# Expert loop of a two-block layer: token gather by quarter rows, turned on VectorE, with scatter and pair down halves in turns

## The reference, cut to what matters

```python
def moe(h, w_router, router_bias, w_gate, w_up, w_down, ws_gate, ws_up, ws_down):
    ...
    scores = jax.nn.sigmoid(xt.astype(jnp.float32) @ w_router.astype(jnp.float32))
    ...
    _, eidx = lax.top_k(jnp.where(emask, sel, -jnp.inf), TOP_K)
    ...
    gates = jnp.einsum('mk,mke->me', wts, jax.nn.one_hot(eidx, N_EXPERTS, dtype=wts.dtype)).astype(h.dtype)

    def expert_block(args):
        x_b, g_b = args
        hg = jnp.einsum('td,edf->tef', x_b, w_gate)
        hu = jnp.einsum('td,edf->tef', x_b, w_up)
        return jnp.einsum('tef,efd->td', jax.nn.silu(hg) * hu * g_b[..., None], w_down)
    ...
    shared = (jax.nn.silu(xt @ ws_gate) * (xt @ ws_up)) @ ws_down
    return (routed.reshape(M, D) + shared).reshape(B, T, D)
```

## Time and profile before

| what | us |
|---|---|
| median of 3 runs (1544.88 to 1546.15) | 1545.85 |
| span of the profiled execution | 1536.5 |
| median less span (what lies around it) | 9.35 |
| expert loop's repeated part, 15 starts of `pair_in` apart (862.00 to 1505.61) | 643.61 |
| one step of it, mean | 42.91 |

### The profile page before, as it was taken

One profiled execution on the slowest core, in us unless ns is written; L12 is line 12 of the kernel. 1 busy time (PEld: TensorE's weight loads), 2 busy tenths in 40 slices (PEclk: granted clock), 3 DMA queues, 4 the chain that ended last, 5 costly groups with the idle time before them and its releaser, 6 DMA issues. The chain is left out here.

```text
span 1536.5 us, 30699 instructions
## 1 busy us (share of the span) xinstructions
PE 1452.9 (95%) x12703; PEld 1211.8 (79%) x12703; DVE 935.7 (61%) x1479; ACT 660.6 (43%) x943; POOL 146.2 (10%) x254
## 2 busy tenths in 40 slices
PE   6999989999999999978898999999999999999996
PEld 5997878789999999866697677777777777777773
DVE  5653666366776368546767466666656555666564
ACT  4333522346443356615555433444444433344442
POOL 8000000001000001001121011110110111110000
PEclk9999999999999999889999999999999999999998
DMA  7455110254554668435617788899888888899883
GB/s 268 141 205 171 58 62 4 79 196 165 198 187 165 163 122 182 151 108 192 213 36 303 286 331 324 336 354 348 333 343 315 314 341 325 326 355 349 336 335 142
DMA packets 115851, 351.99 MB, mean 229 GB/s; under 512 B 9689, under 2 KB 35504, under 8 KB 99328
## 3 DMA queue, kind: packets, MB, share of 16 engines
q1 hardware_dynamic: 105536, 317.85, 57.5%
q0 software_dynamic: 8064, 26.88, 5.6%
q10 hardware_dynamic: 2112, 5.31, 1.0%
HBM read 346.73 MB, written 3.28 MB: 228 GB/s over the span
## 5 line engine op out<-in xcount | busy, mean ns | idle before, releaser
L3411 DVE TENSOR_TENSOR weights_lo<-raw_weights,weights_hi 128x2048 fp32r<-128x2048 f32 x97 | 219.3, 2288 | 77.6 <-ACT weights_hi L3295 77.6
L3295 ACT ACTIVATE weights_hi<-raw_weights 128x2048 fp32r<-128x2048 f32 x97 | 181.8, 1910 | 20.9 <-DMA raw_weights<-in_w_gate 18.7
L3064 PE MATMUL bank<-x_hi,weights_hi 128*128 128x256 f32 x544 | 154.2, 284 | 1.2 <-DVE weights_lo L3411 1.2
L3065 PE MATMUL bank<-x_lo,weights_hi 128*128 128x256 f32 x544 | 153.9, 283 | 0.0
L3066 PE MATMUL bank<-x_hi,weights_lo 128*128 128x256 f32 x544 | 153.9, 283 | 0.0
L371 PE MATMUL bank<-in_x_hi,in_w_hi 128*128 128x272 f32 (+2 forms) x392 | 116.4, 297 | 3.5 <-DVE in_w_lo L320 3.5
L371 PE MATMUL bank<-in_x_hi,in_w_lo 128*128 128x272 f32 (+2 forms) x392 | 114.2, 291 | 0.0
L371 PE MATMUL bank<-in_x_lo,in_w_hi 128*128 128x272 f32 (+2 forms) x392 | 114.1, 291 | 0.0
L3153 PE MATMUL bank<-raw_weights,gathered_pair 128*64 128x512 f32 x512 | 113.4, 595 | 0.0
L1447 DVE TENSOR_TENSOR ffn_weights_lo<-weight_ring,ffn_weights_hi 128x2048 fp32r<-128x2048 f32 x33 | 75.6, 2292 | 51.9 <-ACT ffn_weights_hi L1442 51.9
L3064 PEld LDWEIGHTS bank<-x_hi,weights_hi 128*128 128x128 f32 x544 | 104.3, 192 | 3.1 <-DVE weights_lo L3411 1.7
(11 more groups left out here) (687 smaller groups left out, 3520.6 us busy)
## 6 DMA issues: line engine op xcount, KB each, us to landing
raw_weights<-in_w_gate SPq DMA_DIRECT2D x64, 1024.0 KB, 8.9
raw_weights<-in_w_up SPq DMA_DIRECT2D x64, 1024.0 KB, 9.5
raw_weights<-in_w_down SPq DMA_DIRECT2D x64, 1024.0 KB, 8.1
weight_ring<-in_w_in SPq DMA_DIRECT2D x17, 2048.0 KB, 9.6
weight_ring<-in_w_ffn_in SPq DMA_DIRECT2D x22, 1024.0 KB, 6.2
mixer_memory<-in_w_ada SPq DMA_DIRECT2D x84, 256.0 KB, 4.0
weight_ring<-in_w_ffn_out SPq DMA_DIRECT2D x5, 2048.0 KB, 7.7
weight_ring<-in_w_out SPq DMA_DIRECT2D x4, 2048.0 KB, 7.7
```

The costliest lines, as they stand in the source:

```text
L3064: T.matmul(out_, hi[:, d, cut], x_hi[:, d, :], start=(d == 0), stop=False)
L3065: T.matmul(out_, hi[:, d, cut], x_lo[:, d, :], start=False, stop=False)
L3295: S.activation(w_hi[:, n % 4, :], raw_w[:, k % RAW, :], ACT.Copy).then_inc(s_hi.sem, 1)
L3411: V.tensor_tensor(w_lo[:, n % 4, :], raw_w[:, k % RAW, :], w_hi[:, n % 4, :].bitcast(F32), ALU.subtract).then_inc(s_lo.sem, 1)
```

## The change

Five things change, all in and just ahead of the expert loop.

1. **Dealt rows.** The copy of the tokens in DRAM is stored with its features in another order (dealt), by four GpSimd copies (L3047 of the changed kernel) and two DMAs on POOL's queue, in place of two DMAs on ScalarE's.
2. **Quarter rows.** Each gathered tile is fetched by four indirect DMAs of 128 pieces of 1 KB, in place of one of 128 pieces of 4 KB: eight for a step. The piece numbers (four times the token plus a quarter) must be spread over the partitions; that takes two small VectorE products (`row_parts`), a TensorE product of 8 columns (`spread_rows`), and a VectorE addition (`row_index`).
3. **The turn.** One VectorE 32x32 transpose of 128x1024 for each tile (`turn_single`, `turn_pair`) takes the place of TensorE's 16 transposes and of ScalarE's eight copies; `gathered_hi` and `gathered_lo` are now one operation each on 128x1024, both from SBUF.
4. **Order on TensorE.** The halves of the single scatter and of `pair_down` stand in turns, and so do the halves of the pair scatter and of the next dense gate product.
5. **Order elsewhere.** `spreads(i + 1)` moves ahead of `rest_of(n + 5)`. On POOL the next rank rows and `gate_of` come behind the eight gathers. For the first step, `spread_rows(0)` stands ahead of `down(0)`, and the two turns and `got_lo(0)` behind `hidden_lo(1)`.

The core of the diff:

```diff
+    quarter_rows = tokens_dram.rearrange("t (a e) -> (t a) e", a=4)
...
                 for i in range(STEPS):
...
+                    pool.wait_ge(s_rows_ix.sem, s_rows_ix.count(i + 1))
+                    if i == 0:
                         pool.wait_ge(s_xback.sem, 4)
                         pool.wait_ge(s_xt_out.sem, 32)
                     else:
-                        pool.wait_ge(s_got.sem, 4 * i)
-                    for j in range(2):
-                        pool.indirect_dma_start(xg[:, j, :], None, tokens_dram[:, :],
-                                                bass.IndirectOffsetOnAxis(ap=slot_token[:, j:j + 1], axis=0)).then_inc(s_xg.sem, 16)
+                        pool.wait_ge(s_got_m.sem, s_got_m.count(i))
+                        pool.wait_ge(s_got_p.sem, i)
+                    for j, landed in enumerate((s_xg_m, s_xg_p)):
+                        for b in range(4):
+                            pool.indirect_dma_start(xg[:, j, b * T2:b * T2 + T2], None, quarter_rows,
+                                                    bass.IndirectOffsetOnAxis(ap=row_of_slot[:, 4 * j + b:4 * j + b + 1], axis=0)
+                                                    ).then_inc(landed.sem, 16)
                     if i == 0:
                         pool.wait_ge(s_rows_out.sem, 16)
                         gate_of(1)
+                    if i + 1 < STEPS:
+                        pool.wait_ge(s_put.sem, 12 * (i + 1))
+                        rows_of(i + 1)
+                        gate_of(i + 2)
...
+                spread_rows(0)
                 down(0)
+                product(1, 0)
                 for i in range(STEPS):
-                    product(i + 1, 0)
                     product(i + 1, 1)
-                    if i == 0:
-                        for q in range(4):
-                            gather(0, q)
                     single_in(i)
+                    if i + 1 < STEPS:
+                        spread_rows(i + 1)
                     down(i + 1)
                     single_turn(i)
                     pair_in(i)
                     single_down(i)
                     pair_turn(i)
+                    scatter(i, put_m, 4 * i + 1, 0)
+                    pair_down(i, 0)
+                    scatter(i, put_m, 4 * i + 1, 1)
+                    pair_down(i, 1)
+                    scatter(i, put_p, 4 * i + 3, 0)
                     if i + 1 < STEPS:
-                        gather(i + 1, 0)
-                    scatter(i, put_m, 4 * i + 1, s_one_put)
+                        product(i + 2, 0, 0)
+                    scatter(i, put_p, 4 * i + 3, 1)
                     if i + 1 < STEPS:
-                        gather(i + 1, 1)
-                    pair_down(i)
-                    if i + 1 < STEPS:
-                        gather(i + 1, 2)
-                        gather(i + 1, 3)
-                    scatter(i, put_p, 4 * i + 3, s_pair_put)
+                        product(i + 2, 0, 1)
...
+                def turn_single(i):
+                    dve.wait_ge(s_xg_m.sem, 64 * (i + 1))
...
+                    V.transpose(xm, blocks_of[:, 0]).then_inc(s_got_m.sem, 1)
+
+                def turn_pair(i):
+                    dve.wait_ge(s_xg_p.sem, 64 * (i + 1))
...
+                    V.transpose(xp[:, :, :], blocks_of[:, 1]).then_inc(s_got_p.sem, 1)
...
+                    if more:
+                        turn_single(i + 1)
                     for half in range(2):
                         out_lo(half, 4 * i + 1)
                     if more:
-                        got_lo(i + 1, 0)
+                        turn_pair(i + 1)
                         rest_of(n + 6)
-                        got_lo(i + 1, 1)
+                        got_lo(i + 1)
                     for half in range(2):
                         out_lo(half, 4 * i + 3)
```

More of the change, by code:

```diff
@@ L3176, in scatter @@
-                def scatter(i, put, ready, done):
-                    pe.wait_ge(s_put.sem, 12 * i + 2)
-                    for half in range(2):
-                        pe.wait_ge(s_ylo.sem, ready + half)
-                        for c in range(2):
-                            for y in (y_hi, y_lo):
-                                mm = T.matmul(bank[2 * c + half][:, :], put[:, i % 2, c * P:c * P + P], y[:, half * 512:half * 512 + 512],
-                                              start=False, stop=False, skip_group_check=True)
-                        if half == 0 and i == STEPS - 1 and put is put_p:
-                            s_left.on(mm)
-                    mm.then_inc(done.sem, 1)
+                    pe.wait_ge(s_ylo.sem, 4 * i + 1 + half)
@@ new lines, in pair_down, with scatter @@
+                    cut = slice(half * 512, half * 512 + 512)
+                    for f in range(2):
+                        for j, lanes in enumerate(HALF):
+                            mm = T.matmul(bank[5 + half][lanes, :], ht_p[:, f, lanes],
+                                          piece_view(raw_w[:, (k + j) % RAW, :], 2)[:, f, cut], start=(f == 0), stop=(f == 1))
+                    mm.then_inc(s_pair_down.sem, 1)
+                def scatter(i, put, ready, half):
+                    pe.wait_ge(s_put.sem, 12 * i + 2)
+                    pe.wait_ge(s_ylo.sem, ready + half)
+                    for c in range(2):
+                        for y in (y_hi, y_lo):
+                            mm = T.matmul(bank[2 * c + half][:, :], put[:, i % 2, c * P:c * P + P], y[:, half * 512:half * 512 + 512],
+                                          start=False, stop=False, skip_group_check=True)
+                    if half == 0 and i == STEPS - 1 and put is put_p:
+                        s_left.on(mm)
+                    if half == 1:
+                        mm.then_inc((s_one_put if put is put_m else s_pair_put).sem, 1)
@@ L3560, in _ @@
                 token_lo(3)
+                row_index(0)
                 rest_of(4)
@@ L3573, in _ @@
                     if i == 0:
-                        for q in range(4):
-                            got_lo(0, q)
+                        turn_single(0)
+                        turn_pair(0)
+                        got_lo(0)
+                    if more:
+                        spreads(i + 1)
                     rest_of(n + 5)
+                    if more:
+                        row_index(i + 1)
                     dve.wait_ge(s_one_sig.sem, i + 1)
```

164 lines of the change are left out of this document (89 added, 75 removed).

## The result

The changed kernel takes 1621.54 us (median of 4 runs, 1615.0 to 1625.3); the kernel before took 1545.37 us beside it. The ratio is 1.0495, with a 95% interval of 1.0441 to 1.0549: slower by 76 us. The time lies in the predicted range, 16.6 us above the predicted 1605.

The account below looks back on a forecast made before the run. The prediction took the loop as bounded by TensorE's work and, almost level, the chain over piece n+6's load. Adding 14 + 13.5 + 22.5 + 9 = 59 us to a 1536.5 us span, plus 9.35 around it, gave 1604.9 us; range 1566 to 1624.

Parts of the forecast that it names:

- longer chain: From piece n+6's landing to the pair scatter: 6.1 us instead of 5.34, making steps 0.95 us longer, 14 us in all.
- landing of piece n+6: Gathers and rank rows on the DMA engines delay this load by 0.9 us a step, 13.5 us in all.
- clock: TensorE idles 2.7 to 3.6 us before the pair scatter; its lowered clock costs 1.5 us a step, 22.5 in all.
- first step: At the loop's start, eight gathers ahead of gate_of(1) delay single_in(0) to about 859: 9 us more.
- What bounds the kernel: In the loop, TensorE's 42.75 us a step and the chain over piece n+6's load differ by tenths of a microsecond.
- Rival (d): TensorE stays the loop's bound and the transposes' time is won: steps of 40.5 us, 1521 us in all; chance 0.05.
- The turns on VectorE: The two transposes on VectorE behind pair_in take 1.21 us each, hidden, and cost nothing.
- The gathers: POOL issues eight a step at 1.27 us each, the last at P + 6; just hidden, with traffic costing 0.9 us.
- I take the row, 0.9: Traffic cost per step, from an earlier step with late gathers that took 43.68 us in place of 42.75; bounds 0 and 2.
- Rival (a): TensorE's clock holds, as it reaches its wait later or idles too briefly: 1582 us; chance 0.18.
- the 9.35 us between its span and its median: Time added around the forecast span of 1595.5 us to reach 1604.9 us.
- Rival (c): POOL's issues or the pair's gathered quarters come late, so the second turn delays rest_of(n+6): 1620 to 1635 us; chance 0.15.

Follow-up runs that it names:

- a2: Changed kernel with the three rank-row DMAs on POOL held back until piece n+6 has landed; 1583.69 us, ratio 1.0254 to the kernel before.
- a4: Changed kernel with 14 unused filler products in TensorE's idle time between pair_down and the pair scatter; 1601.42 us, ratio 1.0358 to before.
- b1: Kernel before without TensorE's gather transposes of steps 1 to 15 and their copies and cut; 1533.55 us, ratio 0.9931.
- a9: Changed kernel with five combined reorderings, plus pair_in doing gate then up columns, and got_lo(0) ahead of the pair's turn; 1533.37 us, ratio 0.993 to before.
- a1: Changed kernel with got_lo(i + 1) on VectorE moved behind the two out_lo of the pair; 1609.35 us, ratio 1.0409 to before.
- a7: Changed kernel without the four GpSimd copies that deal the token rows; 1618.47 us, ratio 1.0481 to before.
- b2: Kernel before with pair_in doing one expert's 16 products after the other's, signalling after each half; 1622.26 us, ratio 1.0495.
- b3: b1 with pair_in doing one expert's 16 products after the other's, signalling after each half; 1616.88 us, ratio 1.0459 to before.

## Why the prediction was right or wrong, point by point

| term of the sum | forecast, us | measured, us | from |
|---|---|---|---|
| longer chain | 14 | 16.5 | a2 less the clock, against before |
| landing of piece n+6 | 13.5 | 24.2 | changed kernel against a2, less the clock |
| clock | 22.5 | 18.0 | work over 620.0; a4 |
| first step | 9 | 18.2 | 25.0 less 6.8 ahead of the changed code |
| sum | 59 | 76.9 | medians: 76.2 |

The time is 16.6 us above the forecast and 2.5 below the upper end of the range. Three terms were too small, by 2.5, 10.7 and 9.2 us, and the clock's was too large by 4.5; that this one offset a part of the others is luck.

- **What bounds the kernel: right.** The chain over piece n+6 was nearly tied with TensorE's work; b1 shows it at 42.5 us and a9 shows the other bound by itself. Rival (d) named the right condition (an earlier landing of n+6); its size was off. The transposes are worth 1.87 us of a step and not 2.5, since the 1.58 us in the earlier trace rows held waiting, and what is added is 0.41 (41.35 less 40.94) and not 0.25 (`spread_rows` is two products of 0.23 us). The floor was 41.35, not 40.5.
- **The chain: right, 6.1 us** from the landing to the pair scatter: 952.29 - 946.18 = 6.11. a1 shows `got_lo` in it. Over the loop it came to 2.5 us more than forecast.
- **The turns on VectorE: right.** 1.238 and 1.234 us at a forecast of 1.21, hidden. The figure of the Trainium skill (VectorE: DVE Perf Modes, section "The three transpose paths") is for one 128x128 tile in 16 bits; the 2.5 us that I had estimated from it don't hold for a turn of 128x1024 in float32: the measurement decides.
- **The gathers: the pace was right, the traffic mis-sized.** POOL's pitch is 0.95 + 0.30 us for 1 KB pieces as for 4 KB ones (1.27 forecast), and the last is issued at 935.64, P + 4.7 (6 forecast). The load of n+6 took 7.17 us in the step shown, 4.7 to 7.5 over the steps, against 5.02. The step that failed is "I take the row, 0.9": that row was a step in which the gathers alone came late; the rank rows went out at P + 29 in before, and now at P + 6:

```profile
935.64 0.95 POOL L3074 DMA_INDIRECT gathered_rows<-tokens_scratch,row_of_slot  x1 [0.30 <-issue]
936.59 0.60 POOL L3059 DMA_DIRECT2D kept<-rows_scratch  x1
937.17 1.10 POOL L3061 DMA_DIRECT2D kept<-rows_scratch  x2
```

  Piece n+6 is issued behind them, at 938.99. Measured: 24.2 / 15 = 1.6 us a step, nearer to my upper bound of 2 (which was itself rounded down: 0.75 MB at 335 GB/s are 2.3 us).
- **The clock: right in kind, a little too large.** I counted 1.5 us in all 15 steps; 11 fell, losing 1.4 to 2.3 us, and four did not. Rival (a) was thus true in a quarter of the steps. a4 shows that the idle time is the cause. The Trainium skill (TensorE: Matmul & The Clock Gate, section "HAM oscillation — how this bites in real kernels") tells of a loop that waits about 3 to 5 us in every tile and loses the clock each time. I had carried that over to a wait of 2.7 us and more. The changed kernel's trace agrees for its ten waits of 4.2 us and more, each followed by a fall; the waits of a2, 2.3 to 2.6 us, are shorter than the ones in that section, and 12 of its 15 steps keep 1.00.
- **The first step: half of it missed.** `single_in(0)` starts 35.2 us behind `put_single(0)`, 12.0 more than before, where the forecast had 8.6. `put_single(0)` itself is 10.5 us later than before in this profile (6.8 of it ahead of the changed code), so the first gather, at 843.0, is where the forecast's 832 would put it. But four of the eight took 1.9 to 2.8 us to issue, not 0.97:

```profile
843.01 2.83 POOL L3074 DMA_INDIRECT gathered_rows<-tokens_scratch,row_of_slot  x1 [13.77 <-DVE row_of_slot L3477]
...
857.75 0.60 POOL L3055 DMA_DIRECT2D kept<-rows_scratch  x1
```

  so `gate_of(1)` goes out at 857.75, 4.9 us later than the forecast's 842.4 + 10.5, and VectorE waits for its row until 864.24. Why those four were slow was not tried. The stretch with the POOL copies, counted as nothing ("at most 3"), took 3.7 more in this pair of profiles (some 3 in the mean, see a7). TensorE, idle for 11.00 us, then starts `single_in(0)` at the lower clock (granted 0.82 up to `pair_in`), 2.6 us, which I had not counted. 12.0 + 3.7 + 2.6 = 18.3.

```profile
864.24 0.69 DVE L3441 TENSOR_TENSOR kept<-kept 128x512 f32<-128x512 f32 x1 [6.72 <-DMA kept<-rows_scratch]
872.88 0.77 PE L3148 MATMUL bank<-weights_hi,gathered_hi 128*128 128x512 f32 x1 [11.00 <-DVE put_single L3496]
```

- **Around the span.** The remaining 6.8 us lie ahead of any changed code, where the mixer's product of L2668 starts at 754.28 in the profile of before, and at 758.2 to 767.2 in the thirteen other profiles, b1, b2 and b3 among them, whose code is the same up to there. So the profiled execution of before was a quick one. That fits with the 9.35 us between its span and its median, which I carried over as if they lay around the span: in the changed kernel the profiled execution took 1621.99 us with a span of 1620.3, so only 1.7 lie around it. Why that stretch varies was not tried.
- **Rival (c) fell:** no turn waited for a gather, though the times of the whole (1620 to 1635) were its own. A time in a rival's range is not yet the rival's mechanism; the zero in the idle column of the turns decides.

## What to carry to other kernels

Where two bounds are nearly tied, the gain of relieving one is the distance to the other, here 0.4 of 1.9 us; find what the other hangs on (here one load, issued when one slot comes free) and move that first or together. A background transfer that used to go out at a quiet time is a cost as soon as it stands ahead of the load at the head of the chain. An idle time that grows a little can also take the clock with it: here 24.2 us of longer waiting brought 13.5 us at the lower clock.

## What the runs showed of the hardware

- **Products on different halves of the columns overlap.** Thirty-two products of 512 columns, each on 64 columns of the array, took 7.09 us in turns and 12.29 us in line, a factor of 1.7. The Trainium skill, "TensorEngine Tiling (Array Packing)", section "Key Properties", says that different tiles can do their weight loads and products in parallel; the traces agree for the two column halves, and add that the order of the instructions decides it. Cutting each into two of 256 columns, in turns, cost nothing (64 in 7.13 us, a9).
- **VectorE beside a POOL copy.** In the start of the loop some short operations took 0.86, 0.75 and 0.68 us where the same ones take 0.23, 0.25 and 0.25 without the copies (a7):

```profile
814.69 2.13 POOL L3047 COPY gathered_pair<-gathered_rows 128x512 f32<-128x512 f32 x2 [6.75 <-ACT gathered_rows L3357]
```

```profile
814.62 0.20 DVE L3566 TENSOR_SCALAR raw_weights<-raw_weights 128x64 f32<-128x64 f32 x1
814.85 0.86 DVE L3567 TENSOR_TENSOR raw_weights<-raw_weights 128x64 f32<-128x64 f32 x1
815.75 0.23 DVE L3569 MAX8 raw_weights<-raw_weights 128x8 f32<-128x64 f32 x1
```

  Single operations within the copies take 0.4 to 0.6 us more, others within the same copies don't.
- **The clock and idle time, in this loop:** behind 2.3 to 2.6 us of idle time it held in 12 steps of 15 (a2) and fell in 3 of the same size; in the changed kernel it held behind 2.3, 2.6, 3.0 and 3.2 us, fell behind another 3.0, and fell each of the ten times behind 4.2 us and more. In a1 it fell behind 2.06 us and held behind 3.21, and in a4 it fell behind 1.96; in b1 it held behind 1.3 to 1.6 us in all 15 steps. Length alone doesn't decide between about 2.0 and 3.2 us; what does stays open.
- **A 32x32 transpose by VectorE** of 128x1024 float32 takes 1.24 us, as long as a two-operand operation of that size (1.22).
